# Scores and values of an attention as three fp32r products each, on one Trainium2 core

## What is computed

```python
q = q.reshape(Bsz, S, G, HPG, DH) * (DH ** -0.5)
s_c = einsum('btghd,bcgd->bghtc', q, kcc) + bias_c      # short branch, 15 keys
s   = einsum('bqghd,bgqkd->bghqk', qc, kg) + bias       # selected branch, causal
s_w = einsum('bjqghd,bjkgd->bjghqk', qw, kwb) + bias_w  # window branch, causal
# each: masked softmax p, then p @ values of the same branch
o = gates[0] * o_c + gates[1] * o_s + gates[2] * o_w
h = h + o @ w_out
```

## Time and profile before

| | us |
|---|---|
| median of 3 runs (2104.7 to 2104.82) | 2104.81 |
| the profiled execution | 2104.84 |
| its span in the profile | 2103.1 |

### The profile page before, as it was taken

The page is one execution under the profiler, slowest core; times in us unless marked ns, Lnnn a source line. Parts: engine busy times, 40 slices in busy tenths (PEclk is TensorE's granted clock), DMA queues, the critical chain, the costliest instruction groups (busy, mean ns, idle before and its releaser), DMA issues.

```text
span 2103.1 us, 29342 instructions
## 1 busy us (share of the span) xinstructions
PE 2094.3 (100%) x10132; PEld 1765.1 (84%) x10132; DVE 1268.8 (60%) x1715; ACT 1010.7 (48%) x1342; POOL 77.1 (4%) x141
## 2 busy tenths in 40 slices
PE   9999999999999999999999999999999999999998
PEld 8888888888888888888888888888888888888887
DVE  7767666555555555545556866857757655455464
ACT  6465665544444444444444555444454454444444
POOL 1001221000000000000000000000000000000000
PEclk9999999999999999999999999999999999999999
DMA  8576444656566556656665555555555556556564
GB/s 299 189 269 232 143 131 162 209 196 204 199 209 199 199 199 199 209 192 201 200 202 192 188 183 186 187 177 179 190 176 183 176 184 206 192 199 201 190 241 148
DMA packets 112823, 411.28 MB, mean 196 GB/s; under 512 B 12802, under 2 KB 12842, under 8 KB 112352
## 3 DMA queue, kind: packets, MB, share of 16 engines
q1 hardware_dynamic: 106848, 386.97, 55.5%
q0 software_dynamic: 5744, 23.07, 3.2%
q10 hardware_dynamic: 144, 0.03, 0.0%
HBM read 394.01 MB, written 2.14 MB: 188 GB/s over the span
## 4 chain that ended last, share of the span: by engine, by line
PE 99%; DMA 0%; ACT 0%; DVE 0%; DVEq 0%; SPq 0%; issue 0%
PE set L1655 24%; PE set L1657 24%; PE set L1656 24%; PE set L1681 13%; PE set L1689 7%; PE misc L1929 1%; PE misc L1808 1%; PE set L1779 1%; PE misc L1881 1%; PE misc L1868 1%; PE misc L2057 0%; PE set L1783 0%; PE misc L1854 0%; PE set L1739 0%; PE misc L1882 0%; PE misc L2026 0%
## 5 line engine op out<-in xcount | busy, mean ns | idle before, releaser
L948 DVE TENSOR_TENSOR w_hl<-raw,w_hl 128x1024 fp32r<-128x1024 f32 x729 | 891.9, 1225 | 737.4 <-ACT w_hl L579 735.4
L579 ACT ACTIVATE w_hl<-raw 128x1024 fp32r<-128x1024 f32 x729 | 770.9, 1059 | 960.9 <-PE set L1657 776.8
L1655 PE MATMUL set<-w_hl,x_hl 128*128 128x512 f32 x1408 | 553.3, 393 | 0.0
L1657 PE MATMUL set<-w_hl,x_hl 128*128 128x512 f32 x1408 | 548.5, 390 | 0.0
L1656 PE MATMUL set<-w_hl,x_hl 128*128 128x512 f32 x1408 | 547.8, 389 | 0.0
L1657 PEld LDWEIGHTS set<-w_hl,x_hl 128*128 128x128 f32 x1408 | 264.3, 188 | 55.7
L1656 PEld LDWEIGHTS set<-w_hl,x_hl 128*128 128x128 f32 x1408 | 264.4, 188 | 54.4
L1655 PEld LDWEIGHTS set<-w_hl,x_hl 128*128 128x128 f32 x1408 | 264.3, 188 | 54.1
L1681 PE MATMUL set<-x_hl,w_hl 128*128 128x512 f32 x1216 | 295.4, 392 | 0.0
L1681 PEld LDWEIGHTS set<-x_hl,w_hl 128*128 128x128 f32 x1216 | 222.3, 188 | 42.7 <-DVE t L969 0.2
L1689 PE MATMUL set<-x_hl,w_hl 128*128 128x256 f32 x1216 | 163.0, 284 | 0.0
(11 more groups left out here) (332 smaller groups left out, 1732.4 us busy)
## 6 DMA issues: line engine op xcount, KB each, us to landing
raw<-in_weights SPq DMA_DIRECT2D x730, 512.0 KB, 3.4
turn<-f_b POOLq DMA_DIRECT2D x11, 512.0 KB, 3.2
bias_g<-bias POOLq DMA_DIRECT2D x4, 572.0 KB, 3.4
h<-in_x SPq DMA_DIRECT2D x4, 512.0 KB, 7.1
bias<-u_dram POOLq DMA_DIRECT2D x1, 2048.0 KB, 13.8
h<-in_x_rows POOLq DMA_DIRECT2D x1, 2048.0 KB, 11.3
turn<-h POOLq DMA_DIRECT2D x4, 512.0 KB, 3.5
m_turn<-m_t POOLq DMA_DIRECT2D x4, 512.0 KB, 3.1
```

The costliest lines, as they stand in the source:

```text
L579: a(high, whole, ACT.Copy).then_inc(hi_ready, 1)
L948: tt(low, whole, high.bitcast(F32), ALU.subtract).then_inc(lo_ready, 1)
L1655: mm(o, hl[:, kt, 0, x], w[:, 0, c], start=first and k == 0, stop=False, skip_group_check=True)
L1657: last = mm(o, hl[:, kt, 1, x], w[:, 0, c], start=False, stop=True, skip_group_check=True)
```

## The change

Queries and keys are split into high and low parts in fp32r, and so are the turned probabilities and the values. Each of the 4 products of `scores` and of the 4 large ones of `values` becomes three fp32r products of the same columns: high by high, high by low and low by high. The short branch's product stays.

- ACT gets the high parts: `key_high` (four of 128x512, behind the gate projection), `short_key_high`, and `query_high` (one of 128x512 at slots 1 and 7 of each block); `prob_t` comes out as fp32r.
- DVE gets the low parts: `key_low` (four), `short_key_low`, `query_low` (slots 1 and 7), and for each head `low_probs`: two subtractions of 128x384, which read PSUM and `prob_t`, write `prob_lo` and signal `ptl_ready`. They stand at slot 2n for head n-2, behind `take_head`; for the last head at slot 11. PE's `values`, and the transposes of the next head, wait for `ptl_ready` instead of `pt_ready`.
- POOL makes `v_lo` beside `v_g`, and its loop over groups 1 and 2 is written out.
- The high parts `k_hi` and `q_hi` lie where `h` lies, so the load of x by tokens is moved from before the attention to behind the last scores (in group 3, when `scores_done` has reached 16).
- `scores` wait for `ql_ready` (half a group's queries at heads 0 and 2) instead of `taken`.

```diff
 (POOL)
                     for b in range(2):
-                        g.tensor_copy(v_g[:, b, :, :], v_sw[:, b, :, bass.ds(gi * DH, DH)])
+                        v_b = v_sw[:, b, :, bass.ds(gi * DH, DH)]
+                        own.link(g.tensor_copy(v_g[:, b, :, :], v_b))
+                        g.tensor_tensor(v_lo[:, b, :, :], v_b, v_g[:, b, :, :].bitcast(F32), ALU.subtract)
...
+                if n == HPG - 1 and last_group:
+                    pool.wait_ge(scores_done, HEADS)
+                    pool.dma_start(h_rows, d["x_rows"]).then_inc(rows_in, 16)
...
-        pool.dma_start(h_rows, d["x_rows"]).then_inc(rows_in, 16)
...
 (DVE)
+        def low_probs(gi, n):
+            dve.wait_ge(pt_ready, gi * HPG + (n + 1))
+            if real(gi, n - 1):
+                dve.wait_ge(o_done, gi * HPG + n)
+            for b in range(2):
+                last = tt(prob_lo[:, b, :], m[2 + b][:, 0:TRI], prob_t[:, b, :].bitcast(F32), ALU.subtract)
+            last.then_inc(ptl_ready, 1)
+        def head_step(gi, slot):
+            n = slot // 2
+            if slot % 2 == 0:
+                if real(gi, n - 3):
+                    take_head(gi, n - 3)
+                if real(gi, n - 2) and not last_head(gi, n - 2):
+                    low_probs(gi, n - 2)
+            elif last_head(gi, n - 2):
+                low_probs(gi, n - 2)
...
 (PE)
-            mm(m[0][:, 0:K1], q1, keys[:, 0:K1], start=True, stop=True)
-            mm(m[0][:, K1:K1 + KC + P], q0, keys[:, 0:KC + P], start=True, stop=True)
-            mm(m[1][:, KC:K1], q1, keys[:, K1:K1 + S], start=True, stop=True)
-            mm(m[1][:, K1:K1 + P], q0, keys[:, KC + P:K1], start=True, stop=True).then_inc(scores_done, 1)
+            for out, q, keys in ((m[0][:, 0:K1], late, slice(0, K1)), (m[0][:, K1:K1 + KC + P], early, slice(0, KC + P)),
+                                 (m[1][:, KC:K1], late, slice(K1, K1 + S)), (m[1][:, K1:K1 + P], early, slice(KC + P, K1))):
+                mm(out, q_hi[:, n, q], high[:, keys], start=True, stop=False)
+                mm(out, q_hi[:, n, q], low[:, keys], start=False, stop=False)
+                last = mm(out, q_lo[:, n, q], high[:, keys], start=False, stop=True)
...
-            pe.wait_ge(pt_ready, gi * HPG + (n + 1))
+            pe.wait_ge(ptl_ready, gi * HPG + (n + 1))
...
-                mm(m[1][:, 0:S], v_g[:, b, 0, :], prob_t[:, b, 0:S], start=b == 0, stop=False)
-                mm(m[1][:, P:S], v_g[:, b, 1, :], prob_t[:, b, S:TRI], start=False, stop=False)
+                for t, keys_of in ((0, slice(0, S)), (1, slice(S, TRI))):
+                    o = m[1][:, t * P:S]
+                    mm(o, v_g[:, b, t, :], prob_t[:, b, keys_of], start=b == 0 and t == 0, stop=False)
+                    mm(o, v_g[:, b, t, :], prob_lo[:, b, keys_of], start=False, stop=False)
+                    mm(o, v_lo[:, b, t, :], prob_t[:, b, keys_of], start=False, stop=False)
```

More of the change, by code:

```diff
@@ L169, in program @@
     x_hl = sb("x_hl", [P, KT, 2, S], F32R)
+    with ExitStack() as heads_only:
+        k_hi = sb("k_hi", [P, GROUPS, KC + 2 * S], F32R, scope=heads_only)
+        q_hi = sb("q_hi", [P, HPG, S], F32R, scope=heads_only)
     h = sb("h", [P, KT, S])
@@ L185, in program @@
     with ExitStack() as s1:
-        k_all = sb("k_all", [P, GROUPS, KC + 2 * S], scope=s1)
+        with ExitStack() as whole_keys:
+            k_all = sb("k_all", [P, GROUPS, KC + 2 * S], scope=whole_keys)
+        k_lo = sb("k_lo", [P, GROUPS, KC + 2 * S], F32R, scope=s1)
         v_sw = sb("v_sw", [P, 2, TT, GROUPS * DH], scope=s1)
@@ L215, in program @@
             prob = [sb(f"prob{n}", [P, PCOLS], scope=s1c) for n in range(2)]
-            prob_t = sb("prob_t", [P, 2, TRI], scope=s1c)
+            prob_t = sb("prob_t", [P, 2, TRI], F32R, scope=s1c)
             prob_hl = sb("prob_hl", [P, P], F32R, scope=s1c)
@@ L509, in _ @@
         group(0, first=True)
-        with pool.Fori(1, GROUPS - 1) as gi:
+        for gi in range(1, GROUPS - 1):
             group(gi)
@@ L666, in hidden_gelu, with key_high, short_key_high, query_high @@
             a(hid_in[:, n, :], hid_in[:, n, :], ACT.Gelu_apprx_tanh).then_inc(hid_ready, 1)
+        def key_high(g):
+            if g == 0:
+                act.wait_ge(taken, B_KV + 8)
+                act.wait_ge(x_ready, KT)
+            a(k_hi[:, g, KC:], k_all[:, g, KC:], ACT.Copy).then_inc(kh_ready, 1)
+        def short_key_high():
+            act.wait_ge(kvc_ready, 1)
+            a(k_hi[:, :, 0:KC], k_all[:, :, 0:KC], ACT.Copy).then_inc(kh_ready, 1)
+        def query_high(gi, half):
+            act.wait_ge(taken, gi * 2 + (B_Q + half + 1))
+            two = slice(half * HT, (half + 1) * HT)
+            a(q_hi[:, two, :], q_t[:, two, :], ACT.Copy).then_inc(qh_ready, 1)
         splits(Pos(C_G1), 1)
@@ L670, in _ @@
         for n in range(2):
-            splits(Pos(C_VC + 2 * n * NB), 2 * NB, {2: lambda: hidden_gelu(0)} if n else {1: gate_sigmoid})
+            splits(Pos(C_VC + 2 * n * NB), 2 * NB, {2: lambda: hidden_gelu(0)} if n else
+                   {1: gate_sigmoid} | {4 + 2 * g: lambda g=g: key_high(g) for g in range(GROUPS)})
             take_cross(C_VC + 2 * (n + 1) * NB, B_VC + 2 * n, m[3 - n][LOW:LOW + GROUPS * NC, 0:CH],
@@ L710, in attention, with slot_step @@
                 take_pt(gi, n - 2)
+        def slot_step(gi, slot):
+            if slot == 1:
+                query_high(gi, 1)
+            attention(gi, slot)
+            if slot == 7 and not (isinstance(gi, int) and gi == GROUPS - 1):
+                query_high(gi + 1, 0)
         def attentions(gi, slots=NB):
-            return {s: lambda s=s: attention(gi, s) for s in range(slots)}
-        splits(Pos(C_Q), NB, {0: lambda: hidden_gelu(1)}, B_Q, B_Q)
+            return {s: lambda s=s: slot_step(gi, s) for s in range(slots)}
+        splits(Pos(C_Q), NB, {0: lambda: hidden_gelu(1), 6: lambda: query_high(0, 0), 7: short_key_high}, B_Q, B_Q)
         splits(Pos(C_Q + NB), NB, attentions(0), B_Q + 2, B_Q)
@@ L1127, in gates_out, with key_low @@
                ALU.mult).then_inc(gates_ready, 1)
+        def key_low(g):
+            dve.wait_ge(kh_ready, g + 1)
+            tt(k_lo[:, g, KC:], k_all[:, g, KC:], k_hi[:, g, KC:].bitcast(F32), ALU.subtract).then_inc(kl_ready, 1)
         for n in range(2):
-            splits(Pos(C_VC + 2 * n * NB), 2 * NB, None if n else {8: gates_out})
+            splits(Pos(C_VC + 2 * n * NB), 2 * NB, None if n else
+                   {8: gates_out} | {5 + 2 * g: lambda g=g: key_low(g) for g in range(GROUPS)})
             take_tokens(B_VC + n, [v_sw[:, n, t, :] for t in range(TT)], MIX)
@@ L1226, in take_head, with query_low, short_key_low, last_steps @@
             tt(low, src, high.bitcast(F32), ALU.subtract).then_inc(o_ready, 1)
-        def heads_out(gi, slots=NB):
-            return {2 * n: lambda n=n: take_head(gi, n - 3) for n in range((slots + 1) // 2) if real(gi, n - 3)}
+        def low_probs(gi, n):
[14 more added lines that the diff above has]
+                low_probs(gi, n - 2)
+        def query_low(gi, half):
+            dve.wait_ge(qh_ready, gi * 2 + half + 1)
+            two = slice(half * HT, (half + 1) * HT)
+            tt(q_lo[:, two, :], q_t[:, two, :], q_hi[:, two, :].bitcast(F32), ALU.subtract).then_inc(ql_ready, 1)
+        def short_key_low():
+            dve.wait_ge(kh_ready, GROUPS + 1)
+            tt(k_lo[:, :, 0:KC], k_all[:, :, 0:KC], k_hi[:, :, 0:KC].bitcast(F32), ALU.subtract).then_inc(kl_ready, 1)
+        def last_steps(gi):
+            query_low(gi, 0)
+            if isinstance(gi, int) and gi == 0:
+                short_key_low()
+        def heads_out(gi, slots=NB):
+            steps = {slot: lambda slot=slot: head_step(gi, slot) for slot in range(slots)}
+            steps[1] = lambda: query_low(gi, 1)
+            if not (isinstance(gi, int) and gi == GROUPS - 1):
+                steps[7] = lambda: query_low(gi + 1, 0)
+            return steps
         def softmax_step(gi, n):
@@ L1242, in _ @@
         q_scale = DH ** -0.5
[L1243 removed]
+        take_block(Pos(C_Q), B_Q, B_Q, NO_CROSS_Q, q_t[:, :, ::-1], MIX, q_scale, extras={3: hidden, 6: compressed, 7: lambda: last_steps(0)})
         take_block(Pos(C_Q + NB), B_Q + 2, B_Q, NO_CROSS_Q, q_t[:, :, ::-1], MIX, q_scale,
@@ L1846, in scores @@
             if n == 0:
-                pe.wait_ge(taken, gi * 2 + (B_Q + 2))
+                pe.wait_ge(ql_ready, gi * 2 + 1)
+                if isinstance(gi, int) and gi == 0:
+                    pe.wait_ge(kl_ready, GROUPS + 1)
+            if n == HT:
+                pe.wait_ge(ql_ready, gi * 2 + 2)
             if real(gi, n - 1):
```

22 lines of the change are left out of this document (15 added, 7 removed).

## The result

The changed kernel takes 2109.37 us (median of 12 runs), the one before beside it 2104.82: a ratio of 1.0023, 95% interval 1.0015 to 1.0030. The profiled execution took 2109.32 with a span of 2107.6, so 4.5 us more than before. The forecast was 2108.6.

A forecast was written before the change was run, and what follows sets the result against it. PE, busy for 2094.3 of 2103.1 us, was taken to bound the kernel. The sum was 2104.84 + 2.5 (products) + 1.1 (slot 4 of group 0) + 0.2 (last head) = 2108.6 us; likeliest case 2107.6 to 2110.4, whole range 2106 to 2131.

The forecast's parts named there:

- Taken out of PE: Float32 products of scores (1.35 us) and values (1.30) leave PE, together 2.65 us for a head.
- Put into PE: Per head 12 fp32r products for scores and 12 for values; net of those removed, +2.5 us over 16 heads.
- the prediction's own mark of 0.10: Sign in PE's chain: the forecast is wrong if narrow products stand below 0.10 or above 0.13.
- the 12 ns of the moving side: On PE, a product costs about 12 ns more than its columns, so narrow ones were priced 0.113 us, above the 0.11 floor.
- Rivals 1 and 3: Narrow fp32r products cost float32's 0.22 (2130.1 us, chance 0.20), or 0.079 like the transposes (2102.1 us, chance 0.06).
- DVE's new step at slot 4 of group 0: `low_probs` ahead of head 2's share and mask delays PE's first values: +1.1 us, once (0.8 to 1.4).
- The same step for the other heads: `low_probs` and `query_low` fit into DVE's wait for ACT's exponentials, 2.3 us per head, so costed at nothing.
- the prediction's own mark (no more than three heads): Sign on PE's waits: the forecast is wrong if PE waits in more than three heads.
- The last head: `low_probs` ends at 342.7, after PE's values began before at 342.51: +0.2 us (0 to 0.5).
- What is hidden: ACT's query and key splits, `key_low`, POOL's `v_lo` and the moved load of x by tokens were costed at nothing.
- Rival 2: DVE late in every head as POOL and DVE hinder each other: 14 heads x 0.7, 2118.6 us, chance 0.06.
- Rival 4: Matmuls pay by passes alone, three for four: 10.6 us less, 2095.5 us with the stalls, chance 0.02.

## Why the prediction was right, and where only its sum was

The time came out 0.8 above the forecast and inside the likeliest case's own range of 2107.6 to 2110.4. The mechanism held: the products give nothing back, since narrow ones stand on a floor, and DVE's step at slot 4 makes PE wait. Of the sizes, two steps were off in opposite directions.

- **Taken out of PE** and the wide products' prices held: they read 0.12 to 0.13 in the chain. The twelve pieces of scores sum to 1.35, and with the 0.05 in the piece behind them to 1.40, where 1.41 was forecast.
- **Put into PE**: +2.5 forecast, 1.6 measured, below the lower bound of 2.0. The term was the narrow product's 0.113; with its 128 columns it costs the load's 0.11 and no more. In each narrow group the first piece stands at 0.06 or 0.07, outside the prediction's own mark of 0.10, but the piece behind the group is 0.04 to 0.05 longer, so the three together cost 0.33. The argument that the 12 ns of the moving side (10 by its own rows, 0.119 - 0.109) come on top was wrong: load and moving lie beside each other and the longer one counts, as cutting the one and then the other showed. The prediction's sum with 0.11, redone, is 1.9 and not 2.0 (and 3.6, not 3.7, with 0.119); the 0.3 from there to the measured 1.6, 0.02 a head, stays open. Rivals 1 and 3 are out, since narrow products cost neither 0.22 nor 0.079.
- **DVE's new step at slot 4 of group 0**: +1.1 forecast (0.8 to 1.4), 1.6 measured. The queue was right, and with POOL out of the way the wait is 1.09. What was missed is in the "hidden" step: POOL's two more operations were given no price because POOL is idle. They took DVE's time instead.
- **The same step for the other heads**, costed at nothing: 1.0 measured, at five places. The argument watched only the chain exponentials, mask, values. There the cover held: DVE's wait fell to 15.8 us and never to zero (0.24 and 0.28 at the two shortest of the earlier trace rows). But `query_low` and the stretched query operation stand ahead of `take_head` too, and for that PE's next scores wait. By the prediction's own mark (no more than three heads) this step is wrong: seven places wait.
- **The last head**: +0.2 forecast, 0.3 measured. The range of 0 to 0.5 held, but PE does not stand waiting for 0.2, as forecast: it gets there with the low parts, and the 0.3 is the slower start behind a semaphore.
- **What is hidden**: the move of x by tokens cost nothing (the run on it alone); the key and query splits on ACT didn't hold PE up, whose only printed wait from 182 to 350 us is the 1.64 for DVE.
- **Rival 2** (POOL and DVE hinder each other) was the right mechanism with the wrong place: it cost 0.5 at slot 4 and 0.2 at each of two heads, not 0.7 in each head. **Rival 4** and the hope of three passes for four are out for narrow products, but for the wide ones the gain of 0.16 a head in the scores that lay in the earlier trace rows was there to be had.

So -0.9 + 0.5 + 1.0 + 0.1 make the 0.7 between the forecast's 3.8 and the 4.5 of the spans. That the time came so close is partly luck: 0.9 too much on the products stood against 1.6 too little on the waits.

## What to carry to other kernels

Price a product by the longer of two times, that of its moving columns and that of its weight load. Three fp32r products then replace a float32 one with gain only where the moving side is clearly the longer one; here the line runs somewhere between 144 and 256 columns. When a step is put into a queue, look at everything that stands behind it there, at each one's reader, and not just at the chain that looks tight. And give a price to work on an engine that is mostly idle: here POOL's parts cost PE 0.5 us through DVE.

## What the runs showed of the hardware

- The weight load of an fp32r product sets a floor of 0.11 us per matmul; with 32 stationary columns it is gone (0.06 to 0.07), while 32 instead of 128 moving columns change nothing. Float32 products of 8 and of 128 columns at 0.11 a MATMUL fit the same floor, which was not tested for them; the fp32r transposes at 0.079 lie below it.
- DVE operations with two operands in SBUF and POOL's operations beside them hinder each other: two splits of 128x1024 took 3.12 instead of 2.35, a 128x512 one 0.99 instead of 0.69, POOL's subtraction of 128x256 1.59 instead of 0.77. The 32 subtractions that read PSUM took 547 to 560 ns, also at 242.87 us, where POOL worked beside them. The Trainium skill has this as an exclusive lock on a shared pair of ports, which a DVE operation with two inputs in SBUF takes against a GpSimd operation that reads SBUF ("SBUF — State Buffer", section "SBUF: two separate sides"); the rows agree.
- PE's granted clock was 0.50 in the 2 us after a wait of 1.82 (and fell after one of 1.85), and 1.00 after one of 1.64. The two kernels differ in their products too, so that the length of the wait decides is not shown; the cost, 1.6 us, is.
- A matmul that a semaphore releases just as PE gets to it costs 0.16 to 0.27 more than one in a row, with no idle time printed for PE: the wait shows only as a first piece of up to 0.39 instead of 0.12. At the last head its weight load starts at 346.72 together with the product, where the load ahead of it starts at 346.05 for a product at 346.27; that the load held back is what costs the time is likely, and no run tested it.
